# Reordering VectorE, ScalarE and TensorE inside the two-map attention of a fused two-block kernel

## The reference, cut to what matters

```python
def one_block(qs):
    qb1, qb2 = qs
    s1 = jnp.einsum('bqhd,bkhd->bhqk', qb1, k1).astype(jnp.float32) * scale
    s2 = jnp.einsum('bqhd,bkhd->bhqk', qb2, k2).astype(jnp.float32) * scale
    p = jax.nn.softmax(s1, axis=-1) - lam * jax.nn.softmax(s2, axis=-1)
    return jnp.einsum('bhqk,bkhd->bqhd', p.astype(v.dtype), v)
```

```python
for n, o_branch in enumerate((o_mla, o_fnet, o_diff, o_hgrn)):
    gate = jax.nn.sigmoid(gate_logits[..., n * D_MODEL:(n + 1) * D_MODEL].astype(jnp.float32))
    merged = merged + gate.astype(x.dtype) * (o_branch @ w_branch[l, n])
```

## Time and profile before

| | |
|---|---|
| device time, median of 3 runs | 3654.01 us (3652.26 to 3657.74) |
| the profiled execution | 3657.07 us, of which the span of the trace is 3655.3 us |
| busy share of the span | PE 98%, weight loads 80%, DVE 59%, ACT 44%, POOL 2% |
| mean granted TensorE clock | 0.991 of full speed |
| chain that ended last | PE 91%, DVE 5%, ACT 2% |

### The profile page before, as it was taken

The page is one execution under the profiler, slowest core; times in us unless marked ns, Lnnn a source line. Parts: engine busy times, 40 slices in busy tenths (PEclk is TensorE's granted clock), DMA queues, the critical chain, the costliest instruction groups (busy, mean ns, idle before and its releaser), DMA issues.

```text
span 3655.3 us, 52186 instructions
## 1 busy us (share of the span) xinstructions
PE 3577.2 (98%) x18986; PEld 2924.0 (80%) x18986; DVE 2156.8 (59%) x3118; ACT 1604.7 (44%) x2666; POOL 87.2 (2%) x74
## 2 busy tenths in 40 slices
PE   7999999999999999999999999999999999999999
PEld 5888778888998777899867677889986767788997
DVE  6843388426873654687355656478735565647862
ACT  3222432224552554455354544455535454435552
POOL 0000100000000000000000000000000000000000
PEclk9999899999999999999999999999999999999999
DMA  9843278533333222333332222333332222233332
GB/s 313 275 128 96 82 240 279 149 97 93 104 100 98 58 58 58 89 106 97 95 83 65 62 67 64 89 94 104 100 101 74 70 58 73 57 91 93 104 104 87
DMA packets 643163, 388.72 MB, mean 106 GB/s; under 512 B 17968, under 2 KB 602544, under 8 KB 642992
## 3 DMA queue, kind: packets, MB, share of 16 engines
q1 hardware_dynamic: 640256, 381.41, 35.6%
q10 hardware_dynamic: 2736, 4.98, 0.4%
HBM read 384.23 MB, written 2.10 MB: 106 GB/s over the span
## 4 chain that ended last, share of the span: by engine, by line
PE 91%; DVE 5%; ACT 2%; issue 1%; SPq 1%; DMA 0%; POOL 0%; DVEq 0%; ACTq 0%; POOLq 0%
PE bank L2659 20%; PE bank L2660 20%; PE bank L2661 20%; PE bank L2788 6%; PE bank L2790 6%; PE bank L2789 6%; PE bank L2965 1%; PE bank L2946 1%; PE bank L3029 1%; PE bank L2948 1%; PE bank L2947 1%; PE bank L3186 1%; DVE work L2332 1%; PE bank L2985 1%; DVE w_lo L1631 1%
## 5 line engine op out<-in xcount | busy, mean ns | idle before, releaser
L1631 DVE TENSOR_TENSOR w_lo<-stage,w_hi 128x1024 fp32r<-128x1024 f32 x432 | 528.6, 1224 | 837.4 <-ACT w_hi L866 837.1
L2659 PE MATMUL bank<-h_hi,w_hi 128*128 128x512 f32 x2088 | 842.3, 403 | 10.3 <-DVE w_lo L1631 3.0
L2661 PE MATMUL bank<-h_hi,w_lo 128*128 128x512 f32 x2088 | 816.6, 391 | 0.0
L2660 PE MATMUL bank<-h_lo,w_hi 128*128 128x512 f32 x2088 | 816.3, 391 | 0.0
L866 ACT ACTIVATE w_hi<-stage 128x1024 fp32r<-128x1024 f32 x432 | 456.5, 1057 | 750.5 <-PE bank L2661 745.8
L2659 PEld LDWEIGHTS bank<-h_hi,w_hi 128*128 128x128 f32 x2088 | 393.7, 189 | 122.0 <-issue 30.4
L2660 PEld LDWEIGHTS bank<-h_lo,w_hi 128*128 128x128 f32 x2088 | 394.1, 189 | 83.4 <-issue 6.7
L2661 PEld LDWEIGHTS bank<-h_hi,w_lo 128*128 128x128 f32 x2088 | 393.6, 189 | 84.0
L2659 PE MATMUL bank<-a_lo,w_hi 128*128 128x512 f32 x704 | 274.6, 390 | 0.0
L2661 PE MATMUL bank<-a_lo,w_lo 128*128 128x512 f32 x704 | 274.0, 389 | 0.0
L2660 PE MATMUL bank<-a_hi,w_hi 128*128 128x512 f32 x704 | 274.0, 389 | 0.0
(11 more groups left out here) (421 smaller groups left out, 6753.0 us busy)
## 6 DMA issues: line engine op xcount, KB each, us to landing
stage<-in_ffn_w_in SPq DMA_DIRECT2D x176, 512.0 KB, 3.8
stage<-in_w_in SPq DMA_DIRECT2D x108, 512.0 KB, 3.9
stage<-in_w_gate_up SPq DMA_DIRECT2D x88, 512.0 KB, 3.7
ada_stage<-in_ada_w SPq DMA_DIRECT2D x128, 256.0 KB, 4.4
work<-in_ada_w SPq DMA_DIRECT2D x128, 256.0 KB, 6.1
stage<-in_ffn_w_out SPq DMA_DIRECT2D x64, 512.0 KB, 3.7
stage<-in_w_down SPq DMA_DIRECT2D x32, 512.0 KB, 4.1
stage<-in_ffn_w_out SPq DMA_DIRECT2D x32, 384.0 KB, 3.4
```

The lines of the kernel that those rows point to most:

```text
L1631: nc.vector.tensor_tensor(lo, stage[:, slot * WORDS:(slot + 1) * WORDS], hi.bitcast(F32), ALU.subtract).then_inc(w_lo_ready, 1)
L2659: nc.tensor.matmul(dst, wh, chunk(hi, k), start=first and a == 0, stop=False)
L2660: nc.tensor.matmul(dst, wh, chunk(lo, k), start=False, stop=False)
L2661: ins = nc.tensor.matmul(dst, wl, chunk(hi, k), start=False, stop=last and a == len(ks) - 1)
```

## The change

Only the two-map attention is touched. On VectorE, a head becomes `paired(h)`: the low part of the branch weights goes ahead of the third maxima (it stood behind them and the merged sum), the gated product ahead of the second maxima, and `next_weights` behind the merged sum, before the fourth maxima. The two late rotations leave head 0 and stand between the maxima of head 0's own scores; the low part of the first goes there as well, and that of the second stays in head 0 behind `next_weights`. `output_low` moves behind `next_weights`. On ScalarE, the first late high part goes ahead of the first gate's tanh, the second ahead of the transposes' copies, and `branch_high` ahead of `convert`. On TensorE, the last head alone changes: six eighths of the gate run ahead of its first transposes instead of alternating with them. No instruction is added or removed.

```diff
@@ ScalarE
                 if mp == 2:
                     exps(0, range(6))
+                    split_roped(late, 2, 3)
                     gate_tanh(fills)
...
-                        after_gate(fills + h)
+                        if fills + h + 1 not in FIRST_FILLS:
+                            branch_high(fills + h + 1)
+                        convert(MIX_UNIT["gate", fills + h] + 2)
+                        if h == 0:
+                            split_roped(late, 3, 4)
                         copies(h, (0, 1))
                         if not last:
                             exps(h + 1, groups[1])
-                        if h == 0:
-                            split_roped(late, 2, 4)
@@ VectorE
+                def paired(h):
+                    more, f = h + 1 < len(heads), fills + h
+                    inverse_sums(h)
+                    weight(h, 0)
+                    if more:
+                        maxima(h + 1, groups[0])
+                    for b in range(1, TB):
+                        weight(h, b)
+                    gated_product(f)
+                    if more:
+                        maxima(h + 1, groups[1])
+                    if f + 1 not in FIRST_FILLS:
+                        branch_low(f + 1)
+                    if more:
+                        maxima(h + 1, groups[2])
+                    merged_sum(f)
+                    next_weights("gate", f)
+                    if h == 0:
+                        split_low(*late["splits"][3])
+                    if h and h % 2 == 0:
+                        output_low(h - 1)
+                    if more:
+                        maxima(h + 1, groups[3])
...
+                if mp == 2:
+                    for g in (1, 2):
+                        maxima(0, groups[g])
+                        ropes_late(late, (g + 1,))
+                    maxima(0, groups[3])
+                    split_low(*late["splits"][2])
+                    for h in range(len(heads)):
+                        paired(h)
@@ TensorE
-                    if mp == 2:
+                    if mp == 2 and last:
+                        gate(fills + h + 1, 0, 6)
+                        first_turns(h, (0, 1))
+                        gate(fills + h + 1, 6, 7)
+                        first_turns(h, (2, 3))
+                    elif mp == 2:
```

More of the change, by code:

```diff
@@ L2076, in merged, with merged_sum @@
             def merged(f):
+                merged_sum(f)
+                if f + 1 not in FIRST_FILLS:
+                    branch_low(f + 1)
+            def merged_sum(f):
                 g = n.merge + f
@@ L2085, in merged @@
                     nc.vector.tensor_tensor(m, m, gs[:], ALU.add).then_inc(merged_ready, 1)
-                if f + 1 not in FIRST_FILLS:
-                    branch_low(f + 1)
             def squares(items):
@@ L2159, in attention @@
                 merged(fills - 1)
[L2160 to L2170, removed]
-                        weights(h)
[L2172 to L2185, removed]
+                if mp == 2:
[6 more added lines that the diff above has]
+                        paired(h)
+                else:
+                    maxima(0, range(len(groups[0]), TB))
+                    for h in range(len(heads)):
+                        weights(h)
+                        if h == 0:
+                            ropes_late(late, (2, 3))
+                        if h and h % 2 == 0:
+                            output_low(h - 1)
+                        gated_product(fills + h)
+                        next_weights("gate", fills + h)
+                        merged(fills + h)
+                        if h == 0:
+                            for i in (2, 3):
+                                split_low(*late["splits"][i])
+                        if h + 1 < len(heads):
+                            maxima(h + 1, range(TB))
                 output_low(len(heads) - 1)
@@ L2247, in take_late, with ropes_late @@
                 n.taken += 2
-            def ropes_late(r):
+            def ropes_late(r, items):
                 dve.wait_ge(rot_taken, n.taken)
-                for i in (2, 3):
+                for i in items:
                     xc, t = r["chunks"][i], r["turned"][i][0:r["rows"]]
```

## The result

The changed kernel took 3636.28 us (median of 5 runs, 3632.95 to 3640.19), the kernel before 3656.98 (5 runs, 3652.26 to 3659.07). The ratio is 0.9947, 95% interval 0.9934 to 0.9961: 20.7 us faster by the medians, where 20.8 had been summed. The prediction had put the time at 3634. The profiled execution took 3634.29, 22.8 less than that of before.

A forecast was written before the change was run, and what follows sets the result against it. TensorE, busy 98% of the span, bounds the kernel; only its idle time or low clock can be won. 7.36 + 5.77 - 1.2 - 1.54 = 10.4 us a layer, 20.8 in both, put at 3634 us, range 3627 to 3645.

The forecast's parts named there:

- Step 1: Heads 0 to 2: `wb_lo` ahead of the third maxima removes TensorE's waits before the branch, 7.36 us a layer.
- Step 2: TensorE's two low-clock stretches behind the removed waits return to full clock, gaining 5.77 us a layer.
- step 4: Behind the grown wait for an exponential, one low-clock stretch of 3.40 us costs 1.54 us a layer (bounds 0 and 4.30).
- Step 3: VectorE's fourth maxima come late, 0.7 us in head 0 and 0.5 in head 2, costing 1.2 us a layer.
- Step 5: The late rotations fit idle time between maxima of head 0's own scores: cost 0, 0.06 us at most.
- Step 6: TensorE's last head, same matmuls in another order: 0 us, bounds -0.9 and +1.9.
- B: Rival, 7%: the branch goes early but TensorE waits as long for exponentials or weights; no change, 3650 to 3658 us.
- A: Rival, 10%: the grown wait keeps TensorE's clock down as long as before; 7.6 us a layer, 15.3 in all.
- C: Rival, 3%: slower, as late `wb_hi` would hold up `wb_lo` and the maxima behind it; 3668 us at 8 us late.

The follow-up runs named there:

- Experiment 1: The kernel before with only `wb_lo` moved ahead of the third maxima in each head of the two-map attention: 3643.26 us against 3656.59.
- experiment 2: The kernel before with only the late rotations (with their high and low parts) moved between the maxima of head 0's own scores: 3647.52 us against 3656.59.
- experiment 6: The kernel of experiment 4 with two eighths of the next gate on TensorE ahead of head 2's first scores: 3627.01 us against 3654.53.
- Experiment 4: The changed kernel with next weights, second late low part and output copy moved ahead of the third maxima: 3633.26 us against 3656.59 for the kernel before.
- experiment 3: The changed kernel with TensorE's last head in its old order, gate pieces between the first transposes: 3634.6 us against 3656.59 for the kernel before.
- experiment 5: The changed kernel with the gate weights' low part computed twice in head 0, ahead of the fourth maxima: 3635.14 us against 3654.53 for the kernel before.

## Why the prediction was right, step by step

*Step 1, the branch no longer waits: right.* 2.1 us to spare had been worked out, and it is 2070.88 - 2068.77 = 2.1. All three waits are gone. Experiment 1 shows that the order alone does most of it, experiment 2 that the rotations' 2.65 us count too.

*Step 2, the clock of the old stretches comes back: right*, less what step 4 gives away. The kernel of experiment 6 has no low stretch in its attentions, and there PE's busy time is 67.92 us against 73.66 before: 5.74 less in the first layer, where 5.77 had been summed.

*Step 3, the fourth maxima are next: right in kind and size.* 0.7 us late was worked out and 0.68 measured, the wait 2.4 and 2.37. In head 2, 0.5 was worked out; the maxima came at 2109.08 for scores begun at 2107.66, so 0.42. Experiment 4 removes this and gets the 1.68 back. By steps 1 and 3 together the idle time was to fall by 6.16 us a layer, and it fell by 6.06 and 6.09.

*Step 4, the clock behind the grown wait: the term that was mis-sized.* I took one low stretch of 3.40 us by its nearest row. It was 6.8 us, in both layers of both profiles of the changed kernel and of experiment 3. At 0.454 of the 6.62 us of work in it that is 3.0 us instead of 1.54, and against experiment 6 the busy time is in fact 2.86 more. These 1.5 us account for the gap between 10.4 and the 8.94 of the first layer. In the second layer the same error is half hidden, since its attention before was 0.59 us longer than the 83.80 counted. So the signs that I had named for this step failed: the attentions took 74.9 and 74.7 us and not 73 to 74, with a mean clock of 0.95 and not over 0.97. The attentions gave 18.7 us, not 20.8; the other 2 of the 20.7 between the medians lie outside the changed stretch, where executions of unchanged code differ by several us. That 20.7 met 20.8 is luck.

*Step 5, the rotations cost nothing: right.* The idle time ahead of head 0's maxima fell from 1.63 to 0.31 and ahead of the reciprocal from 0.92 to 0.32, and the maxima lie where they lay: the scores of head 1 begin 11.44 us behind those of head 0, in both kernels.

*Step 6, the last head: right*, about 0, by experiment 3. The 1.86 us that TensorE idled there before is 15.80 less 13.94, at a clock of 1.00. One sign of being wrong did come up: the first transposes of the last head start 5.56 us behind its last scores (2113.22 and 2107.66), before 5.27 (2126.06 and 2120.79). But in TensorE's old order, in experiment 3, it is 5.53, so the new order isn't what delays them; the late maxima of step 3 stand ahead of these weights in both.

*The durations of step 3: right, though the row is misread.* Step 3 counts VectorE's instructions from start to start, and the prediction goes for this by a row with two instructions 0.60 us apart (2075.20 and 2075.80). It calls them equal-sized and 0.68 long each, but only the first is: the second is `w_lo`, 128x1024 and 1.22 long. The distances hold in the changed kernel. Merged sum (0.68 long) and `w_lo` start 0.60 apart (2071.78, 2072.38), the late low part (0.68 long) and the maxima too (2073.51, 2074.11), and the 0.68 of lateness fits these distances.

*The rivals.* B (handed on to the next wait) is true of 1.1 us of 7.4, as step 3 had it, and of no more. A (the clock doesn't recover) is half true: half the old stretch's length stayed, and the 18.7 us of the attentions lie between its 15.3 and the forecast's 20.8. C had no trace: VectorE waited for `wb_hi` in no head.

## What to carry to other kernels

On an engine that works through its list in order (before, `wb_hi` was ready at 2070.41 and `wb_lo` ran at 2078.73, behind all that stood ahead of it), look at what stands ahead of the one instruction that the bound engine waits for, and ask of each piece whether it has a gap of its own elsewhere. A move is finished only when the gap that it opens (1.80 us ahead of the third maxima) has been used for what now stands in the next maxima's way. And a short wait on TensorE was worth more than its length here, because 3.4 us at a clock of 0.50 followed it (experiment 4): covering a wait of 1.68 us with two eighths of a gate gave 2.0 us in each layer. Only 0.7 of them were idle time, since small waits came up behind; 1.3 were clock.

## What the runs showed of the hardware

- The clock fell behind some short waits of TensorE and not behind others, and the length of a wait doesn't say which. In these attentions a wait of 2.34 to 2.37 us was followed by 6.8 us at 0.50 six times in six. One of 3.60 was followed by 6.8 in one layer and 3.4 in the other, one of 1.68 by 3.4 in both (experiment 4). The two waits of 2.19 and 1.68 us around head 0's branch in experiment 1 gave two stretches of 3.4 in one layer and one of 10.2 in the other, and so did those of 1.8 and 1.68 in experiment 2. The 1.82 ahead of head 2's branch was followed by 3.4 four times in four (before and experiment 2), but the 1.82 to 1.90 ahead of the last head's transposes by none, six times in six (before, experiments 2 and 3). What decides isn't settled by these runs.
- Idle time that fell into a low stretch cost less than its length: in the first layer of experiment 5 the wait was 1.23 us longer, 1.29 us of the stretch fell on it, and the attention took 0.6 us more.
- The stretch ahead of the first attention, which no kernel here changes, took 2053.21 us before and 2049.01 in the changed kernel, with the same matmuls and a clock of 0.99 against 1.00. Behind it the unchanged stretches agree to 0.1 us over all nine profiled executions (826.6 to 826.7 us between the attentions, 607.1 to 607.2 behind the second), so the differences between these executions outside the attentions came from it, and the length of the changed stretch in the trace is the better measure of a change of this size.
